# Transposing the cached key pages on VectorE and scoring them in sixteen 32x32 tiles of TensorE, with two pieces of side work placed two tiles later

## What is computed

```python
def fox_sample(q, k_new, v_new, lf_new, k_past, v_past, lf_past):
    ...
    s_past = jnp.einsum('bqhd,bkhd->bhqk', q, k_past).astype(jnp.float32) * scale
    s_past = s_past + suf[:, :, None, :] + c_new[:, :, :, None]
    ...
    p = jax.nn.softmax(jnp.concatenate([s_past, s_new], axis=-1), axis=-1).astype(v_new.dtype)
    out = (jnp.einsum('bhqk,bkhd->bqhd', p[..., :n_past], v_past)
           + jnp.einsum('bhqk,bkhd->bqhd', p[..., n_past:], v_new))
```

## Time and profile before

| what | value |
|---|---|
| median of three runs | 3358.1 us |
| span of the profiled execution | 3354.0 us, 4.1 us less than that median |
| PE busy in the span | 3234.5 us (96%) |
| DVE, ACT, GpSimd busy | 39%, 33%, 15% |
| `sample_fox` on PE | from 645 to 1243 us after the span's start |
| DMA engines' mean share while keys and values both load | 0.93 |

### The profile page before, as it was taken

How to read it: one execution, slowest core, us unless ns; L and a number is a source line. 1 busy time by engine, 2 the same in 40 slices (tenths; PEclk the granted TensorE clock), 3 DMA queues, 4 the chain that set the end, 5 groups by cost and what they waited for, 6 DMA issues and landing times. The chain is left out here.

```text
span 3354.0 us, 51636 instructions
## 1 busy us (share of the span) xinstructions
PE 3234.5 (96%) x19705; PEld 2772.9 (83%) x19705; DVE 1297.8 (39%) x2582; ACT 1096.0 (33%) x2157; POOL 511.4 (15%) x769
## 2 busy tenths in 40 slices
PE   7999999999999998999999999997999999996999
PEld 7999999777777777878888887886999888785887
DVE  4331223232333215545555554333222246655332
ACT  3112232122322225455666653222223244112211
POOL 3310000101111112244433330000000012211000
PEclk9999999999999999989999999999999999997999
DMA  5444533579899964443332225432333544756431
GB/s 158 126 135 144 163 110 120 162 229 304 298 325 310 305 183 141 128 126 89 92 92 85 89 73 169 132 104 82 121 108 102 172 127 145 228 162 210 132 110 56
DMA packets 409588, 515.69 MB, mean 154 GB/s; under 512 B 50855, under 2 KB 298216, under 8 KB 407919
## 3 DMA queue, kind: packets, MB, share of 16 engines
q1 hardware_dynamic: 386503, 444.68, 42.7%
q0 software_dynamic: 22848, 67.78, 6.2%
HBM read 388.50 MB, written 124.22 MB: 153 GB/s over the span
## 5 line engine op out<-in xcount | busy, mean ns | idle before, releaser
L420 ACT ACTIVATE z_st_p<-bank 128x512 f32<-128x512 f32 (+3 forms) x322 | 166.8, 518 | 643.5 <-PE bank L393 641.7
L393 PE MATMUL bank<-h00hi,w_hi_p 128*128 128x352 f32 x960 | 317.4, 331 | 3.9 <-DVE h00lo L1165 3.5
L1829 PE MATMUL bank<-w_hi_o,b_hi_o 128*128 128x512 f32 x782 | 305.6, 391 | 14.0 <-DVE w_lo_o L1755 14.0
L393 PE MATMUL bank<-h00hi,w_lo_p 128*128 128x352 f32 x960 | 309.3, 322 | 0.0
L393 PE MATMUL bank<-h00lo,w_hi_p 128*128 128x352 f32 x960 | 309.1, 322 | 0.0
L1830 PE MATMUL bank<-w_hi_o,b_lo_o 128*128 128x512 f32 x782 | 305.4, 390 | 0.0
L1831 PE MATMUL bank<-w_lo_o,b_hi_o 128*128 128x512 f32 x782 | 305.3, 390 | 0.0
L835 PE MATMUL bank<-pT_fa,v_fa 128*128 128x256 f32 x1092 | 272.0, 369 | 4.4 <-issue 2.4
L393 PE MATMUL bank<-h01hi,w_hi_p 128*128 128x512 f32 x640 | 266.7, 417 | 0.0
L336 DVE CAST w_hi_p<-w_raw_p 128x1024 fp32r<-128x1024 f32 x128 | 89.0, 696 | 422.1 <-PE bank L393 392.9
L393 PE MATMUL bank<-h01hi,w_lo_p 128*128 128x512 f32 x640 | 251.3, 393 | 0.0
(11 more groups left out here) (341 smaller groups left out, 6862.6 us busy)
## 6 DMA issues: line engine op xcount, KB each, us to landing
k_raw_sf<-in_cache_fox_k SPq DMA_DIRECT2D x128, 512.0 KB, 5.3
v_raw_sf<-in_cache_fox_v POOLq DMA_DIRECT2D x128, 512.0 KB, 6.0
z<-z_st_p SPq DMA_DIRECT2D x112, 512.0 KB
w_raw_p<-in_fox_w_in SPq DMA_DIRECT2D x80, 512.0 KB, 5.2
b_raw_o<-bT SPq DMA_DIRECT2D x32, 768.0 KB, 6.2
w_raw_p<-in_pool_w_in SPq DMA_DIRECT2D x48, 512.0 KB, 5.1
out<-tok_p SPq DMA_DIRECT2D x64, 256.0 KB, 4.2
w_raw_o<-z SPq DMA_DIRECT2D x62, 256.0 KB, 2.8
```

The lines of the kernel that those rows point to most:

```text
L393: last = nc.tensor.matmul(bank[:, 0:width], wt[:, u, k, :], h[:, k, at0:at0 + width], start=(m == 0), stop=(m == MM - 1))
L420: nc.scalar.activation(z_st[0:rows_t, t % 2, at0:at0 + width], bank[0:rows_t, 0:width], tiles[t][2]).then_inc(z_read, 1)
L1829: nc.tensor.matmul(bank(t, half)[:, :], bh, w_hi, start=(k == 0), stop=False)
```

## The change

The keys are no longer transposed by PE. DVE transposes a whole page, [128 x 1024], in one instruction that turns each 32x32 block by itself, from `k_raw` straight into `kT`. So the head width lies no longer on 128 partitions but is cut into four pieces of 32 (`x`) along the free dimension, and the 128 tokens of a page into four groups of 32 on the partitions (`y`). Scores are made for a group of four pages, a quad, at every fourth step: for each of four pieces x and two heads g sharing a column group, PE runs 16 small matmuls with 32 rows and 32 columns of weights and 128 moving columns (4 pages of 32 tokens), one for each tile of the array (row group y, column group j), and sums eight of them in each of four PSUM banks (`S_BANKS[y]`). That is 128 matmuls a quad. The queries are needed in the same cut; four more loads (`q4`) and ACT activations (`qx4`) bring them. DVE adds the bias in four instructions of 128 columns a quad instead of two of 256. ACT's and DVE's copies of the transposed keys are gone. `k_raw` has three buffers instead of four, the output bank is single, and `kT`'s second half serves for the queries of the new keys at the start. The plan of `sample_fox` ends at NT+35 instead of NT+33, and those of `prompt_memory` and `prompt_gates` begin two tiles later and end where they ended.

```diff
@@ -2030,2 +2030,2 @@
-    JT, CT, NP2, NV = 4, 32, PAGES // 2, PAGES + 1
-    KR, VR = 4, 4
+    JT, CT, NV = 4, 32, PAGES + 1
+    KR, VR, Q, B = 3, 4, 4, 32
@@ -2034 +2034 @@
-    T_BANKS, S_BANK, O_BANKS, M_BANK = banks[0:2], banks[2], banks[3:5], banks[5]
+    S_BANKS, O_BANK, M_BANK = banks[0:4], banks[4], banks[5]
@@ -2036,2 +2036,2 @@
-    q_raw, g_all, out_all, kn_raw = (c.sb(n, [P, FH, NS]) for n in ("q_raw", "gate", "out_all", "kn_raw"))
-    qx = c.sb("qx", [P, DB, FH, CT])
+    g_all, out_all = (c.sb(n, [P, FH, NS]) for n in ("gate", "out_all"))
+    q4, qx4 = c.sb("q4", [P, FH * Q, NS]), c.sb("qx4", [P, 2, FH, Q, CT])
@@ -2039 +2039,4 @@
-    kT = c.sb("kT", [P, 2, FH, 2 * P])
+    kT = c.sb("kT", [P, 2, Q, FH, Q, B])
+    start = kT[:, 1, :, :, :, :].rearrange("p y h x k -> p (y h x k)")
+    qx = start[:, 0:DB * FH * CT].rearrange("p (b h r) -> p b h r", b=DB, h=FH)
+    q_raw, kn_raw = (start[:, DB * FH * CT + n * FH * NS:DB * FH * CT + (n + 1) * FH * NS].rearrange("p (h n) -> p h n", h=FH) for n in range(2))
@@ -2043 +2046 @@
-    mx, nm, rs, rr = c.sb("mx", [P, 2, NP2 + 1]), c.sb("nm", [P, 2]), c.sb("rs", [P, 2]), c.sb("rr", [P, 2])
+    mx, nm, rs, rr = c.sb("mx", [P, 2, PAGES + 1]), c.sb("nm", [P, 2]), c.sb("rs", [P, 2]), c.sb("rr", [P, 2])
@@ -2053 +2056 @@
-    kt_d, ka_d, kv_d, s_done, sc_d = (c.sem(n) for n in ("k_transposed", "kT_front_copied", "kT_back_copied", "scores_done", "scores_biased"))
+    kt_d, q4_in, q4_d, s_done, sc_d = (c.sem(n) for n in ("k_transposed", "queries_spread", "queries_split", "scores_done", "scores_biased"))
@@ -2071 +2074 @@
-    def pair(s):
+    def quad(s):
@@ -2073,2 +2076,2 @@
-        g = s // 2 - 1
-        return divmod(g, NP2) if s % 2 == 0 and 0 <= g < DB * NP2 else None
+        g = s // Q - 1
+        return divmod(g, PAGES // Q) if s % Q == 0 and 0 <= g < DB * PAGES // Q else None
@@ -2104,0 +2108,2 @@
+                for n in range(Q):
+                    sp.dma_start(q4[B * n:B * (n + 1), :, :], zT[0:D, cols].rearrange("(x k) n -> k x n", k=B)).then_inc(q4_in, 16)
@@ -2106 +2111 @@
-            for x in ([i] if i < KR else [s + KR - 1] if s + KR - 1 < NPG else []):
+            for x in ([i] if i < KR else [s + KR - 1] if 1 <= s < NPG - KR + 1 else []):
@@ -2108 +2113 @@
-                    sp.wait_ge(kt_d, 2 * (x - KR + 1))
+                    sp.wait_ge(kt_d, x - KR + 1)
@@ -2113 +2118 @@
-                sp.wait_ge(zero_d, 4)
+                sp.wait_ge(zero_d, 5)
@@ -2152 +2157,2 @@
-                nc.gpsimd.memset(qx[:, :, :, :], 0.0).then_inc(zero_d, 1)
+                nc.gpsimd.memset(qx, 0.0).then_inc(zero_d, 1)
+                nc.gpsimd.memset(qx4[:, :, :, :, :], 0.0).then_inc(zero_d, 1)
@@ -2197,13 +2203,5 @@
-            if 0 <= s < NPG:
-                pe.wait_ge(k_in[s % KR], 16 * (s // KR + 1))
-                for n, copied in enumerate((ka_d, kv_d)):
-                    if s:
-                        pe.wait_ge(copied, s)
-                    for h in range(4):
-                        last = nc.tensor.transpose(T_BANKS[n][:, h * P:(h + 1) * P], k_raw[:, s % KR, (4 * n + h) * P:(4 * n + h + 1) * P], ident[:, :])
-                    last.then_inc(kt_d, 1)
-            if pair(s) is not None:
-                b, n = pair(s)
-                G = NP2 * b + n
-                pe.wait_ge(ka_d, 2 * G + 2)
-                pe.wait_ge(kv_d, 2 * G + 2)
+            if quad(s) is not None:
+                b, n = quad(s)
+                G = PAGES // Q * b + n
+                pe.wait_ge(kt_d, Q * (G + 1))
+                pe.wait_ge(q4_d, 2 * (b + 1))
@@ -2211,5 +2209,9 @@
-                    pe.wait_ge(sc_d, G)
-                for g in range(2):
-                    for j in range(JT):
-                        h = 2 * j + g
-                        last = nc.tensor.matmul(S_BANK[CT * j:CT * (j + 1), 0:2 * P], qx[:, b, h, :], kT[:, G % 2, h, :], start=(g == 0), stop=(g == 1))
+                    pe.wait_ge(sc_d, Q * G)
+                for m in range(2 * Q):
+                    g, x = divmod(m, Q)
+                    for y in range(Q):
+                        at = slice(B * y, B * (y + 1))
+                        for j in range(JT):
+                            h = 2 * j + g
+                            last = nc.tensor.matmul(S_BANKS[y][CT * j:CT * (j + 1), 0:P], qx4[at, b % 2, h, x, :], kT[at, G % 2, :, h, x, :],
+                                                    start=(m == 0), stop=(m == 2 * Q - 1))
@@ -2219,2 +2221,2 @@
-                if p == 0 and b >= 2:
-                    pe.wait_ge(o_d, b - 1)
+                if p == 0 and b:
+                    pe.wait_ge(o_d, b)
@@ -2225 +2227 @@
-                    last = nc.tensor.matmul(O_BANKS[b % 2][CT * j:CT * (j + 1), 0:2 * P], pT[:, p, CT * j:CT * (j + 1)],
+                    last = nc.tensor.matmul(O_BANK[CT * j:CT * (j + 1), 0:2 * P], pT[:, p, CT * j:CT * (j + 1)],
@@ -2235 +2237 @@
-                act.wait_ge(zero_d, 4)
+                act.wait_ge(zero_d, 5)
@@ -2240,5 +2242,10 @@
-            if 0 <= s < NPG:
-                act.wait_ge(kt_d, 2 * s + 1)
-                if s % 2 == 0 and s >= 4:
-                    act.wait_ge(s_done, s // 2 - 1)
-                nc.scalar.copy(kT[:, s // 2 % 2, 0:4, s % 2 * P:(s % 2 + 1) * P], T_BANKS[0][:, :].rearrange("p (h n) -> p h n", h=4)).then_inc(ka_d, 1)
+            for b in ([0, 1] if i == 1 else [batch(s, -13)]):
+                if b is not None and (b >= 2 or i == 1):
+                    if b == 0:
+                        act.wait_ge(q4_in, 16 * Q)
+                    if b >= 2:
+                        act.wait_ge(s_done, PAGES // Q * (b - 1))
+                    for g in range(2):
+                        nc.scalar.activation(qx4[:, b % 2, :, :, :].rearrange("p (j g) x r -> p g j x r", g=2)[:, g, :, :, TN * g:TN * (g + 1)],
+                                             q4[:, :, :].rearrange("p (j g x) n -> p g j x n", g=2, x=Q)[:, g, :, :, TN * b:TN * (b + 1)],
+                                             ACT.Copy, scale=SCALE).then_inc(q4_d, 1)
@@ -2272,7 +2279,8 @@
-                dve.wait_ge(kt_d, 2 * s + 2)
-                if s % 2 == 0 and s >= 4:
-                    dve.wait_ge(s_done, s // 2 - 1)
-                nc.vector.tensor_copy(kT[:, s // 2 % 2, 4:8, s % 2 * P:(s % 2 + 1) * P], T_BANKS[1][:, :].rearrange("p (h n) -> p h n", h=4)).then_inc(kv_d, 1)
-            if pair(s) is not None:
-                b, n = pair(s)
-                G = NP2 * b + n
+                G = s // Q
+                dve.wait_ge(k_in[s % KR], 16 * (s // KR + 1))
+                if s % Q == 0 and G:
+                    dve.wait_ge(new_d if G == 1 else s_done, 1 if G == 1 else G - 1)
+                nc.vector.transpose(kT[:, G % 2, s % Q, :, :, :].rearrange("p h x k -> p (h x k)"), k_raw[:, s % KR, :]).then_inc(kt_d, 1)
+            if quad(s) is not None:
+                b, n = quad(s)
+                G = PAGES // Q * b + n
@@ -2282,4 +2290,6 @@
-                dst = sc[:, b % 2, n * 2 * P:(n + 1) * 2 * P]
-                nc.vector.tensor_tensor_reduce(out=dst, in0=S_BANK[:, 0:2 * P], in1=dst, scale=1.0, scalar=LOWEST, op0=ALU.add, op1=ALU.max,
-                                               accum_out=mx[:, b % 2, n:n + 1]).then_inc(sc_d, 1)
-                if n == NP2 - 1:
+                part = sc[:, b % 2, n * Q * P:(n + 1) * Q * P].rearrange("p (x y k) -> p y x k", x=Q, y=Q)
+                for y in range(Q):
+                    dst = part[:, y, :, :]
+                    nc.vector.tensor_tensor_reduce(out=dst, in0=S_BANKS[y][:, 0:P].rearrange("p (x k) -> p x k", x=Q), in1=dst, scale=1.0,
+                                                   scalar=LOWEST, op0=ALU.add, op1=ALU.max, accum_out=mx[:, b % 2, Q * n + y:Q * n + y + 1]).then_inc(sc_d, 1)
+                if n == PAGES // Q - 1:
@@ -2287,2 +2297,2 @@
-                                                   op0=ALU.add, op1=ALU.max, accum_out=mx[:, b % 2, NP2:NP2 + 1]).then_inc(bias_d, 1)
-                    dve.wait_ge(sc_d, G + 1)
+                                                   op0=ALU.add, op1=ALU.max, accum_out=mx[:, b % 2, PAGES:PAGES + 1]).then_inc(bias_d, 1)
+                    dve.wait_ge(sc_d, Q * (G + 1))
@@ -2301 +2311 @@
-                nc.vector.tensor_scalar(o_sb[:, :], O_BANKS[b % 2][:, 0:2 * P], rr[:, b % 2:b % 2 + 1], None, ALU.mult).then_inc(o_d, 1)
+                nc.vector.tensor_scalar(o_sb[:, :], O_BANK[:, 0:2 * P], rr[:, b % 2:b % 2 + 1], None, ALU.mult).then_inc(o_d, 1)
@@ -2691 +2701 @@
-                                             [(NT + 2.3, 0), (NT + 4, 3), (NT + 33, 154)], rows.when(NT - 1),
+                                             [(NT + 2.3, 0), (NT + 4, 3), (NT + 35, 154)], rows.when(NT - 1),
@@ -2694,2 +2704,2 @@
-                    prompt, _ = prompt_memory(0, sems, room, z0, 3 * D, 3 * D + XW + D, [(NT + 33, 0), (NT + 33.1, 1), (NT + 33.5, 1), (NT + 41, 42)], rows.when(NT + XQ - 1), ends_f)
```

(3 more changed lines are left out.)

## The result

The changed kernel takes 3502.8 us (median of 4 runs, 3495.8 to 3506.4) where the kernel before takes 3356.9 (3352.6 to 3361.2): 1.0434 of it, with a 95% interval of 1.0418 to 1.0449. It is 146 us slower; 62 us faster was forecast, and the time lies outside the range. The profiled execution has a span of 3498.5 us.

What follows compares the result with a forecast made beforehand. PE's queue was taken as the bound, then page transfers: 3354.0 - 92 (167 lost, 75 gained) + 25 transfers + 0 start + 5 memory attention = 3292 us of span, so 3296 us predicted, range 3257 to 3335 us.

Steps and rivals of the forecast that it cites:

- the quad's price: PE's 128 small matmuls a quad: issue-bound at 2.2 us, 2.35 us with one more switch of the array's form.
- rival 5: Further wait in sample_fox from late key pages, DVE or PE's instructions: 0.2 us a page, 22 us more; chance 0.10.
- The array's price: What quads add to PE's queue in sample_fox: 2.35 us each, 32 x 2.35 = 75 us.
- The rivals' figures: Costs for a quad's small matmuls: row groups taking turns, 7.0 us a quad; a fixed 34 ns a record, 8.7 us.
- Rivals 3 and 4: Slower quads on PE: row groups take turns, 3425 us, chance 0.07; fixed price per small matmul, 3479 us, chance 0.04.
- The transfers as the new bound: In sample_fox's page steps, DMA at share 1.02 makes PE wait 0.23 us a page, 25 us over 108 pages.
- Memory attention two tiles later: Thinner cover of projection matmuls raises PE's waits at its transposes from 6.2 to 11 us: +5, from 0 to +18.
- The start: First pages of sample_fox: the old 5.6 us wait goes, the first quad's takes its place: nothing, -8 to +4.
- VectorE's transpose: DVE's 128 x 1024 key transpose a page: taken as 1.2 us, with DVE staying free.
- PE's loss: Key transposes leaving PE's queue in sample_fox: 1.31 us a page, 128 x 1.31 = 167 us in all.

Runs made afterwards that it cites:

- e1: Changed kernel with each quad's 128 matmuls cut into four pieces of 32, one at each of four steps: 3369.5 us, 1.0038 of the kernel before.
- e4: Kernel before with 128 more tiny float32 matmuls (4 moving columns, no row groups) at every fourth step: 3620.2 us, 1.0783 of the kernel before.
- e7: Changed kernel without cached page loads after the first three of keys and four of values: 3406.4 us, 1.0153 of the kernel before.
- e2: Kernel before with only the change's three moved plans: 3368.1 us, 1.0037 of the kernel before.

## Why the prediction was wrong, point by point

The step that failed is the quad's price, **"I take the issue price, 2.2 us"**, and in it the silent assumption that PE has its instructions when it wants them. I named the true cause in rival 5 ("PE's longer program is brought in too slowly at 512 instructions in 2.2 us"), but priced it with two others at 0.2 us a page, 22 us in all, and in no relation to a row. It was 0.9 us a page in gaps alone. The account, in spans, from the forecast's 3292 us to the 3498.5 measured:

1. **Gaps for instructions:** 108.8 + 5.3 = 114 us, forecast nothing. Shown: they go when the same work is spread (e1), come in another kernel with the same number of instructions (e4), and shrink with the load of the DMA engines (e7).
2. **The low clock after them:** about 57 us, forecast nothing, worked out and not measured by itself. By blocks the quads cost 276 us in all (the blocks of before and after differ by 120 us, with 167 lost and 11 of the plans taken out); less 114 of gaps, 9 of waits for VectorE and 32 x 3.5 of free-running quads, 41 are left; the distances of the projection matmuls outside the blocks add 16 us to what they had before. Rows from 777 to 791 show one case of it. From 640 to 1345 us the granted clock falls to 0.5 thirty times, each time within a stop or up to 2 us behind it, and PE works 142 us at that clock, where the kernel before has a single fall. At half speed those 142 us would cost 71, so 57 is of the right size.
3. **The array's price:** a free-running quad is 1.84 us for its first half with the switch, and 4 x 0.42 more for the second, 3.5 us in all; forecast 2.35. That adds 37 us. The rivals' figures were too high: 13 to 14 ns a record, not 34, and not the 25 that the rule of the Trainium skill's page "TensorEngine Tiling (Array Packing)", section "Instruction Overhead", would give if every record paid it in turn: with that reading the trace disagrees. Rivals 3 and 4, which had a slower kernel (3425 and 3479 us), had the right direction by the wrong cause: row groups do overlap, and a record is cheap.
4. **The transfers as the new bound:** 25 us forecast, none came. PE was never fast enough, and the DMA share stayed at 0.72 where 1.0 was forecast.
5. **Memory attention two tiles later:** forecast +5, it costs 13 (e2); its own waits rose by 6.8 as the step had it, and 6 us more went elsewhere.
6. **The start:** forecast 0. PE waits 5.4 + 1.5 us there and once 7.5 us at 966 us, where SP stood 12.6 us for PE's line 380 with the key loads behind it: some 9 us more than the 5.6 of the earlier trace rows.
7. **VectorE's transpose:** 1.23 us, forecast 1.2, and no bound, as forecast. **PE's loss** of 167 us is used in the account above as forecast; no run takes it off alone.

-25 + 114 + 57 + 37 + 8 + 9 = 200 of the 206 us; the other 6 stay open. The evidence was there beforehand: the page of before lists 158 instruction packets, and in its trace none starts closer than 8.7 us behind another, while two of them a quad were to be taken in 2.2 us. Nothing in that trace showed such a rate; I should have bounded it, as I bounded the row groups.

## What to carry to other kernels

Price a block of small matmuls three times: by streaming, by issue, and by how fast its instructions come in. A burst of more than some 200 pairs of matmul and load records in 3 us stops PE here however little data it has. Bursts of 128 pairs stop it at times (33 us of gaps in all), and pieces of 64 pairs between long matmuls hardly (16 us). Where a change trades few large matmuls for many small ones, spread them first, and count what each piece costs before taking the saving for real: here the pieces took some 142 of 167 us, and the gaps and waits that were left took the rest.

## What the runs showed of the hardware

- PE's program comes in packets of 16384 B, whose data take 0.98 us (median of 85 from 640 to 1345 us in the kernel after) and never start closer than 3.24 us to each other there, nor than 3.28 in any experiment. So no run showed more than 256 instructions in 3.2 us sustained.
- With pages' packets around, the median stop of over 1 us with a packet was 4.1 us; with a DMA share of 0.22 it was 1.5.
- In the stop shown PE stood still from 777.56; the granted clock was 1.00 up to 777, 0.50 from 780 on, and 0.50 until 789 while PE worked again from 783.68 on: 1.2 GHz for 5 us of work. All 30 falls of the clock from 640 to 1345 us in that kernel came with a stop.
- Sixteen 32 x 32 tiles with 128 float32 columns: the first 32 MATMUL records behind other work take 0.318 us (9.9 ns each), the next 32 take 0.465 us, later ones 0.40 to 0.42 us per 32 (13 ns); with four column groups of 128 rows it is 27 ns each. The Trainium skill ("Advanced Engine Details and Errata", "Engine Queue Depths") gives TensorE a queue of 64, "complicated with tiling"; the step behind 32 records, 64 with their loads, would fit it, but no run tested it.
